# A 64-byte shift of the one-hot weights and the raw weights' tile in a two-layer transformer kernel

## What is computed

```
s1, s2 = q[..., :128] @ sub_k1.T, q[..., 128:] @ sub_k2.T      # 8 heads, 128 keys each
experts, gates = the best 16 of the 16 x 16 pairs of (i1, i2), softmax of their scores
a   = einsum('cd,chkd->chk', x, expert_u[experts])
w   = gelu(a) * gates
out = einsum('chk,chkd->cd', w, expert_v[experts])
```

## Time and profile before

| | |
|---|---|
| time, median of 3 runs | 1700.52 us (1700.25 to 1700.53) |
| the profiled execution's own time | 1699.94 us |
| its span, first to last instruction | 1698.1 us |
| TensorE matmuls, busy | 1685.6 us (99%), 11357 of them |
| TensorE weight loads, busy | 1530.1 us (90%) |
| VectorE busy | 1236.4 us (73%) |
| ScalarE busy | 920.0 us (54%) |
| GpSimd busy | 382.4 us (23%) |
| granted TensorE clock | 0.999 of full speed |

### The profile page before, as it was taken

The page is one execution under the profiler, slowest core; times in us unless marked ns, Lnnn a source line. Parts: engine busy times, 40 slices in busy tenths (PEclk is TensorE's granted clock), DMA queues, the critical chain, the costliest instruction groups (busy, mean ns, idle before and its releaser), DMA issues.

```text
span 1698.1 us, 31095 instructions
## 1 busy us (share of the span) xinstructions
PE 1685.6 (99%) x11357; PEld 1530.1 (90%) x11357; DVE 1236.4 (73%) x2436; ACT 920.0 (54%) x1449; POOL 382.4 (23%) x172
## 2 busy tenths in 40 slices
PE   9999999999999999999999999999999999999998
PEld 8897999899999999988888888868899988899997
DVE  6748749876555656578888887976689956769974
ACT  6568664555555555533334334585466645566653
POOL 1130077437777777400000000000000000000000
PEclk9999999999999999999999999999999999999999
DMA  7661665587777777777777896725555564445552
GB/s 309 198 235 38 199 198 170 197 229 216 216 216 214 211 216 218 244 244 240 241 243 238 284 324 204 266 88 206 186 173 195 193 202 143 162 149 195 188 204 72
DMA packets 120454, 346.56 MB, mean 204 GB/s; under 512 B 13328, under 2 KB 45200, under 8 KB 118928
## 3 DMA queue, kind: packets, MB, share of 16 engines
q1 hardware_dynamic: 118480, 336.70, 61.7%
q10 hardware_dynamic: 1856, 8.23, 1.4%
HBM read 321.03 MB, written 23.86 MB: 203 GB/s over the span
## 4 chain that ended last, share of the span: by engine, by line
PE 95%; ACT 2%; DVE 1%; issue 0%; DMA 0%; POOL 0%; ACTq 0%; DVEq 0%
PE banks L879 60%; PE bank L879 33%; PE bank L1287 1%; ACT wsplit L1694 0%; DVE wsplit L2161 0%; ACT probs L1846 0%; ACT H L1728 0%; PE banks L1287 0%; PE bank L934 0%; DMA X<-x 0%; ACT H L1734 0%; PE bank L1145 0%; PE banks L1096 0%; POOL wsplit L1671 0%; PE bank L946 0%
## 5 line engine op out<-in xcount | busy, mean ns | idle before, releaser
L879 PE MATMUL banks<-HT,wsplit 128*128 128x256 f32 (+2 forms) x3542 | 429.6, 282 | 1.3 <-POOL wsplit L1671 0.6
L879 PEld LDWEIGHTS banks<-HT,wsplit 128*128 128x128 f32 x3542 | 418.5, 188 | 10.3 <-issue 3.4
L1981 ACT ACTIVATE wsplit<-raw 128x1024 fp32r<-128x1024 f32 x252 | 266.6, 1058 | 212.5 <-PE banks L879 201.9
L879 PE MATMUL banks<-wsplit,wexp 128*128 128x512 f32 x1536 | 348.4, 389 | 0.0
L879 PEld LDWEIGHTS banks<-wsplit,wexp 128*128 128x128 f32 x1536 | 288.3, 188 | 59.7
L879 PE MATMUL bank<-HT,wsplit 128*128 128x256 f32 (+1 forms) x2694 | 322.2, 278 | 0.0
L879 PEld LDWEIGHTS bank<-HT,wsplit 128*128 128x128 f32 x2694 | 316.4, 188 | 0.0
L1671 POOL TENSOR_TENSOR wsplit<-raw,wsplit 128x1024 fp32r<-128x1024 f32 x114 | 275.0, 2412 | 119.2 <-ACT wsplit L1981 119.2
L1694 ACT ACTIVATE wsplit<-raw 128x1024 fp32r<-128x1024 f32 x146 | 154.3, 1059 | 96.0 <-PE bank L879 48.0
L2161 DVE TENSOR_TENSOR wsplit<-raw,wsplit 128x1024 fp32r<-128x1024 f32 x124 | 151.6, 1235 | 67.2 <-ACT wsplit L1694 66.0
L2744 DVE TENSOR_TENSOR wsplit<-raw,wsplit 128x1024 fp32r<-128x1024 f32 x128 | 156.1, 1219 | 6.0 <-ACT wsplit L1981 6.0
(11 more groups left out here) (333 smaller groups left out, 2021.0 us busy)
## 6 DMA issues: line engine op xcount, KB each, us to landing
raw<-weights SPq DMA_DIRECT2D x148, 512.0 KB, 3.7
raw<-expert_v SPq DMA_DIRECT2D x128, 512.0 KB, 3.6
raw<-expert_u SPq DMA_DIRECT2D x124, 512.0 KB, 4.2
raw1b<-weights SPq DMA_DIRECT2D x102, 512.0 KB, 4.1
raw1a<-weights SPq DMA_DIRECT2D x48, 512.0 KB, 4.2
HT<-acts_parked SPq DMA_DIRECT2D x124, 128.0 KB, 3.4
acts_parked<-act_e SPq DMA_DIRECT2D x62, 128.0 KB, 4.4
acts_parked<-ropeg SPq DMA_DIRECT2D x62, 128.0 KB, 4.2
```

Of the source, the lines that this page charges most:

```text
L879: ins = pe.matmul(out, lhsT, rhs, start=start, stop=stop, **kw)
L1981: act.activation(wsplit[:, s, 0, :], src, ACT.Copy).then_inc(e_hi, 1)
```

## The change

A tensor of 16 words (64 bytes) is declared in front of `hot_a` and `raw0`, and one of 112 words behind `raw0`. `hot_a` and `raw0` go from place 0 to place 64. Everything declared behind moves by 128 words in all, 512 bytes, and keeps its place within 512 bytes. No instruction is added, removed, moved or reshaped on any engine; only addresses differ.

```
--- before.py
+++ after.py
@@ -221,10 +221,12 @@
         ropeg = sb("ropeg", [P, 2, 4, T, 2, 16])
         act_e = sb("act_e", [P, 2, S])
         wexp = sb("wexp", [P, 2, 2, S], F32R)
+        sb("line_before_raw0", [P, 16])
         under_raw0 = ExitStack()
         hot_a = under_raw0.enter_context(nc.sbuf_tensor("hot_a", [P, 2, TOGETHER, NKEYS], F32R))
         under_raw0.close()
         raw0 = sb("raw0", [P, 4, UNIT_COLS])
+        sb("line_after_raw0", [P, 112])
```

## The result

The changed kernel takes 1704.73 us (median of 10 runs, 1704.01 to 1705.71), the kernel before 1700.38 us beside it (median of 10). The ratio is 1.0026, with a 95% interval of 1.0018 to 1.0035: slower by 0.26%. This is rival B of the prediction in kind, not the forecast.

The account below looks back on a forecast made before the run. TensorE, busy 99% of the span, bounds the kernel: matmuls by their pace. 1699.94 - 6.2 (all stretches at 113 ns) + 1.6 (gate products) = 1695.3; the median stands 0.58 higher: 1695.9 us, range 1693.3 to 1708.3.

Parts of the forecast that it names:

- rival B: U stage: groups of gate products leave TensorE at the 118 ns pace from both paces; 1707.5 us, chance 0.30.
- Rival B's pace term: U stage from 385.51 us: all 1176 matmuls at 113 ns go to 118 ns, +5.4 us.
- Rival D: Whole kernel: the change does nothing that TensorE feels, by the two-ports rule; 1700.5 us, chance 0.08.
- Which pace: U stage: which pace TensorE keeps behind a group; the two ends held about level, a little more for 113 ns.
- one condition, 113 to 113, is enough: U stage: a group that leaves the 113 ns pace alone does so 61 times; the 118 ns pace needs two conditions.
- divided matmuls that bring the 113 back: U stage before 385.51 us: divided matmuls restore the 113 ns pace, so these stretches were left out of the sum.
- Term 1: Gate products' own pace in the u stage: 24.4 ns more a group, times 64, +1.6 us.
- The 4.6 for equal places: Loads under a block's last matmul, streamed and loaded both at 64: +4.6 ns, like the step from 113.3 to 117.9.
- The lower bound of the term: Gate products, if the new order of places were the good one: 27 ns a group less, -1.7 us.
- Terms 3 and 4: raw0 at place 64, hidden behind TensorE, and the 512-byte move of everything behind: 0 each.
- The cover that I named for raw0: U stage: POOL's 2.41 us a block against TensorE's 2.72 plus 0.48 a group; 12% slower POOL still hidden.

Follow-up runs that it names:

- e1: Kernel before with raw0 alone moved 64 bytes further in, hot_a left at place 0: 1699.89 us, ratio 1.000.
- e2: Kernel before with only everything declared behind raw0 moved by 512 bytes: 1700.15 us, ratio 1.000.
- e14: Kernel before with hot_a and raw0 moved 32 bytes further in: 1694.46 us, ratio 0.9965.
- e4: Kernel before with hot_a and raw0 moved 128 bytes further in: 1705.54 us, ratio 1.0031.
- e6: Kernel before, hot_a at place 0, groups of gate products made two at a time, back to back, every 3 or 4 blocks: 1706.67 us, ratio 1.0035.
- e13: Kernel before with hot_a split: first product's one-hots loaded from place 0, the other three from 64, raw0 at 0: 1699.19 us, ratio 0.9992.
- e12: Kernel before with hot_a split: first product's one-hots loaded from place 64, the other three from 0, raw0 at 0: 1701.58 us, ratio 1.0008.
- e9: Kernel before, hot_a at place 0, groups at other blocks: one block behind odd groups from 3 on, two or three behind even ones: 1697.54 us, ratio 0.9986.
- e11: Kernel before, hot_a at place 0, groups in pairs with six matmuls between them: 1695.36 us, ratio 0.9973.
- e7: Kernel before with hot_a and raw0 448 bytes further in and a divided matmul behind each group: 1701.10 us, ratio 1.0005.
- e8: Kernel before, hot_a at place 0, HT of the expert step at place 128 instead of 64: 1711.29 us, ratio 1.0064.
- e5: Kernel before with hot_a and raw0 moved 256 bytes further in: 1700.55 us, ratio 1.000.

## Why the prediction was wrong

**Where it held.** The reading of the profile held: TensorE never waits in the stage, the pace has two steady values, a group of gate products is what changes it, and nothing that the change moves outside the u stage matters (e1, e2). Rival B's pace term was 5.4 us and measured 5.0. Rival D, no effect, is out: the interval of the ratio begins at 1.0018. The rule of the Trainium skill (TensorE: Matmul & The Clock Gate, "Step-by-step: what each phase is for"), that a load takes no read bandwidth from the running matmul, does not cover this: one address among otherwise equal programs moved the time by 0.3% either way (e14, e4).

**The step that failed** is the one under "Which pace": "so one condition, 113 to 113, is enough", against two for the 118. Counting conditions is no evidence on how likely each is. In the change a group entered at the 113 leaves at the 118 every time it happens (groups 0, 2 and 4), and from group 5 on a group entered at the 118 leaves at the 118 too: 2496 of the 2520 matmuls behind group 3 and later run at it. The trace before already spoke against the one condition, and I weighed it too lightly: all 34 groups that were entered at the 113 there left at the 118, not one left the 113 alone. TensorE also comes to the 118 after the scores of the expert keys, and the way back at place 0 goes through products that have not settled (128, 117, 125, 113 ns in the list above). e6 shows it: give them four products more, and they settle at 120 and leave at the 118. Of the ten arrangements of the four loads that were run (places 0, 32, 64, 128, 256, 448 and the four split ones), seven gave the alternation, the 118 or a mix; only the three with the first load at 32 kept the 113.

A second step failed beside it: the sum left out the stretches ahead of 385.51, since they "have divided matmuls that bring the 113 back". At place 64 they did not, behind groups 0 and 2; it cost 0.26 us.

**Term 1 had the wrong sign.** "Sum 4.6 + 3 x 6.6 = 24.4 ns a group" came from the 512-column rows. Measured it was -10 ns (480 to 470), -0.65 us and not +1.6. The 4.6 for equal places had no ground in the rows either: 117.9 is a pace of `HT` and `wsplit`, 64 apart, and equal places are the 119.8 of the earlier trace rows. The distance that it stood for was 113 or 115 ns in the change, so nothing was paid. With 256 columns, products streamed at 0 with loads at 64 under them run at 116 to 119 ns from group 4 of the change on, and not at 126; e13, which has only these, saves 16 ns a group. The order of places that costs 6.6 ns with 512 columns gains with 256. The lower bound of the term, -1.7 us, did take it in. With both terms right, B would have read 1700.38 + 5.0 - 0.65 = 1704.7.

**Terms 3 and 4** were right in sum, 0 (e1, e2). The cover that I named for raw0 was used: GpSimd's 30 ns more a block.

**What stays open.** With the first load at 0 or 32 its place decided, whatever the other three had. With it at 64 the other three count too: at 0 two stretches of three are at the 118 (e12), at 64 all from group 4 on. The runs don't show what inside the chip makes 113, 118 and 120 ns, nor why 32 is the good one, nor what a group at 32 does when it is entered at the 118. The period of 256 bytes rests on place 256 alone. Places 96 and 160 were not tried, nor 32 elsewhere in the kernel. Each kernel has one trace; that its other executions have the same pattern is argued from their times, which for each changed kernel lie within 1.7 us of each other.

## What to carry to other kernels

When TensorE is the bound at every moment, look at the distance between starts of equal matmuls, stretch by stretch: two values of one form were a state here, set by the short work that stands between the stretches. The addresses of that short work's first loaded tile are worth a sweep in steps of 32 bytes over 256; each costs one padding line, and here the places 0, 32 and 64 gave 1700.4, 1694.5 and 1704.7 us. Such a state is hard to forecast from one trace, so sweep it rather than argue for one place, and move the disturbances (e9, e11) or reset the state (e7) where the addresses can't be moved, and look whether the reset took, since it did with the first load at 0, 128 and 448 and not at 64.

## What the runs showed of the hardware

- The pace of loaded and streamed 128x256 matmuls depends on where the two operands lie: 113.3 or 117.9 ns with 64 bytes between them, 119.8 with none, 118.8 with 128 (e8).
- It has memory. The same code at the same addresses keeps either of two paces for a whole stretch: 96 matmuls at the 118 at the end of the u stage, 145 at either one in the expert queries, where chance picks it (e6, e9).
- The 118 has kinds that look alike and leave the next group differently (e12; groups 3 and 5 of the change).
- For the place of the loaded tile, 256 bytes further in changed nothing (e5), and 32 bytes did (e14).
- One matmul divided in 24 and 232 columns resets the pace to 113 with `hot_a` at 448 (e7), at about 0.13 us a time: 5.57 us for a two-block stretch against 5.44 without it. It did so at 0 and 128 too, and not with the first load at 64 (25 matmuls in 2.93 us in the change; e12).
- GpSimd's subtraction of a 128x1024 tile takes 2438 ns with the raw tile at place 64 (the change, e1) and 2408 at 0; at 32, 128, 256 and 448 it takes 2404 to 2411.
